# The final normalisation of a routed mixture-of-experts layer: one row tile in each expert step, the rest in one batch behind the steps

## What is computed

```python
y = fourier_mixer(x, w_in, w_out)
h = layer_norm(2 ** 0.25 * x + y, ln_g[0], ln_b[0])
scores = sigmoid(h @ w_router)
group = argmax(sum of the two best (scores + b_router) in each group of 8 experts)
two experts = top_k((scores + b_router)[group], 2);  gate = scores / their sum
y[token] = sum over its two experts e: gate * ((silu(h @ w_gate[e]) * (h @ w_up[e])) @ w_down[e])
out = layer_norm(2 ** 0.25 * h + y, ln_g[1], ln_b[1])
```

## Time and profile before

| | before |
|---|---|
| median of 3 runs | 2350.56 us |
| the profiled execution, and its span | 2350.37 us, 2348.4 us |
| TensorE busy | 2127.3 us (91%) |
| VectorE / ScalarE / GpSimd busy | 1373.1 / 998.2 / 582.7 us |
| HBM traffic | 436 MB, 186 GB/s over the span |

### The profile page before, as it was taken

The page is one execution under the profiler, slowest core; times in us unless marked ns, Lnnn a source line. Parts: engine busy times, 40 slices in busy tenths (PEclk is TensorE's granted clock), DMA queues, the critical chain, the costliest instruction groups (busy, mean ns, idle before and its releaser), DMA issues.

```text
span 2348.4 us, 37687 instructions
## 1 busy us (share of the span) xinstructions
PE 2127.3 (91%) x12222; PEld 1801.6 (77%) x12223; DVE 1373.1 (58%) x2254; ACT 998.2 (43%) x1442; POOL 582.7 (25%) x493
## 2 busy tenths in 40 slices
PE   8999899999999449999999999999999999999600
PEld 3443678888888349999999999999999999998500
DVE  3321148888887746555655656555555565555298
ACT  1221123333233226555555645655455565554143
POOL 1000034444544411211121121212111121211166
PEclk9999999999999769999999999999999999999855
DMA  6880233443333347767776866877677777766376
GB/s 226 283 287 21 67 126 113 147 147 125 116 127 108 126 153 210 222 203 195 219 216 184 248 194 211 227 223 197 180 220 218 219 218 228 209 202 183 98 286 238
DMA packets 136067, 435.59 MB, mean 185 GB/s; under 512 B 30912, under 2 KB 35008, under 8 KB 131904
## 3 DMA queue, kind: packets, MB, share of 16 engines
q1 hardware_dynamic: 98592, 307.12, 38.6%
q0 software_dynamic: 37440, 128.01, 21.6%
HBM read 328.01 MB, written 108.10 MB: 186 GB/s over the span
## 4 chain that ended last, share of the span: by engine, by line
PE 90%; POOL 3%; issue 3%; DMA 2%; DVE 2%; ACT 0%; SPq 0%; POOLq 0%; ACTq 0%; DVEq 0%
PE ps L877 36%; PE ps L901 15%; PE ps L759 15%; PE ps L696 5%; POOL fin_r L1689 3%; PE ps L865 3%; PE ps L741 3%; PE ps L909 2%; PE ps L715 2%; PE ps L793 2%; PE ps L650 1%; PE ps L780 1%; PE ps L700 1%; PE ps L870 1%; PE ps L659 1%
## 5 line engine op out<-in xcount | busy, mean ns | idle before, releaser
L901 PE MATMUL ps<-wd_hi,hidT 128*128 128x512 f32 x1056 | 293.0, 402 | 0.4 <-ACT hidT L1099 0.4
L1359 DVE TENSOR_TENSOR wd_lo<-wraw,wd_hi 128x1024 fp32r<-128x1024 f32 x132 | 161.9, 1226 | 199.0 <-ACT wd_hi L1057 198.7
L901 PEld LDWEIGHTS ps<-wd_hi,hidT 128*128 128x128 f32 x1056 | 190.1, 189 | 36.3 <-ACT hidT L1099 0.8
L1359 DVE TENSOR_TENSOR wg_lo<-wraw,wg_hi 128x1024 fp32r<-128x1024 f32 x132 | 161.4, 1224 | 92.6 <-ACT wg_hi L1057 92.5
L1632 POOL DMA_INDIRECT sums<-yrow_a,ent_now x33 | 57.2, 1733 | 558.4 <-DVE yrow_a L1422 515.4
L1359 DVE TENSOR_TENSOR wu_lo<-wraw,wu_hi 128x1024 fp32r<-128x1024 f32 x132 | 160.7, 1218 | 52.0 <-ACT wu_hi L1057 51.9
L877 PE MATMUL ps<-mxT_hi,wg_hi 128*128 128x256 f32 (+1 forms) x1056 | 163.3, 297 | 13.4 <-issue 13.4
L1099 ACT CAST hidT<-hid 128x320 fp32r<-128x320 f32 x132 | 60.7, 460 | 257.3 <-DVE hid L1440 257.3
L877 PEld LDWEIGHTS ps<-mxT_hi,wg_hi 128*128 128x128 f32 x1056 | 149.7, 191 | 17.9 <-issue 16.0
L877 PE MATMUL ps<-mxT_lo,wg_hi 128*128 128x256 f32 (+1 forms) x1056 | 163.2, 297 | 0.0
L877 PE MATMUL ps<-mxT_hi,wg_lo 128*128 128x256 f32 (+1 forms) x1056 | 162.6, 297 | 0.0
(11 more groups left out here) (212 smaller groups left out, 4120.0 us busy)
## 6 DMA issues: line engine op xcount, KB each, us to landing
wraw<-expert_w_gate SPq DMA_DIRECT2D x132, 512.0 KB, 5.4
wraw<-expert_w_up SPq DMA_DIRECT2D x132, 512.0 KB, 5.4
wraw<-expert_w_down SPq DMA_DIRECT2D x132, 512.0 KB, 4.4
xch<-x SPq DMA_DIRECT2D x16, 1024.0 KB, 6.7
first_stage<-ych SPq DMA_DIRECT2D x16, 1024.0 KB, 8.3
yt<-first_stage SPq DMA_DIRECT2D x16, 1024.0 KB, 4.9
fin_r<-sums SPq DMA_DIRECT2D x32, 512.0 KB, 3.9
out<-fin_r SPq DMA_DIRECT2D x32, 512.0 KB, 2.9
```

Of the source, the lines that this page charges most:

```text
L901: mm = nc.tensor.matmul(psY[h], hidT[:, l, c, t * P:(t + 1) * P], wd[r][:, c, cols], start=(i == c == 0), stop=(i == 2 and c == FC - 1))
L1359: nc.vector.tensor_tensor(piece(1, j), wraw[:, j % SLOTS, :], piece(0, j).bitcast(F32), ALU.subtract).then_inc(wlo_ok, 1)
```

## The change

1. The tokens of each group are written into a list too (four more lists, six list writes in place of four in list_tokens), and VectorE makes a second table (ltab) from the counts of the groups: for each step the number of row tiles that may be taken by then, and where each tile's list begins. The last tile of a group overlaps the one before it. The lists are laid out plainly (a list of 4480 entries for each expert and group) in place of by lanes, so the entries of a step come with three DMAs in place of four; there are 640 and 512 filler rows in place of 128 each.
2. In each step u one tile (lnrow) is normalised: SyncE loads its token numbers, GpSimd gathers its rows from sums in the step before and stores them to out at the end of its own work on the step before's entries; VectorE makes the statistics ahead of its down splits and gain and shift between them; ScalarE makes the root ahead of its first cast. Steps for which no tile is ready work on a dummy of filler rows.
3. The tiles that are left are done in batches of 10: GpSimd gathers all ten, VectorE does statistics and gain and, for even tiles, the shift; for odd tiles ScalarE scales and GpSimd adds the shift. GpSimd stores each by indirect DMA, after the store before it has landed.
4. In a step the second scatter no longer waits for the landing of the first.

```diff
-FB = 8
+LISTS = E + EG
+CAP = 35 * P
+FILL = 512
+FB = 10
...
@@ SyncE: start
-            sp.dma_start(acc[S:S + P, :], x[0:P, :]).then_inc(pad_out, 16)
-            sp.dma_start(hd[S:S + P, :], x[0:P, :]).then_inc(pad_out, 16)
+            sp.dma_start(acc[S:S + FILL + P, :], x[0:FILL + P, :]).then_inc(pad_out, 16)
+            sp.dma_start(hd[S:S + FILL, :], x[0:FILL, :]).then_inc(pad_out, 16)
...
@@ SyncE: expert steps
             load_entries(unit_row(sp, 1))
+            sp.dma_start(lng2, bcast(ln_g[1], P)).then_inc(ln2_in, 16)
+            sp.dma_start(lnb2, bcast(ln_b[1], P)).then_inc(ln2_in, 16)
+            sp.dma_start(lent_in_t, lists[E * CAP:E * CAP + P, :]).then_inc(lent_in, 16)
+            sp.wait_ge(ltab_ok, 1)
+            own_wait(sp, glist_out, 32 * GROUPS, sp_gate)
...
                     load_piece(u, e, j)
+                    if j == 0:
+                        tile = ln_slot(u)
+                        own_wait(sp, lent_ok, u, sp_gate)
+                        load_ln_tile(tile)
...
@@ TensorE: behind the step table
             mm.then_inc(utab_ps, 1)
+            pe.wait_ge(lcol_made, 1)
+            for k in range(2):
+                mm = nc.tensor.matmul(psLtab[:, k * P:(k + 1) * P], lcol[:, k:k + 1], ident,
+                                      start=True, stop=True)
+            mm.then_inc(ltab_ps, 1)
...
@@ ScalarE: a step
+            def ln_deviation(u):
+                act.wait_ge(lvar_ok, u + 1)
+                nc.scalar.activation(lnstd[:, 0:1], lnmv[:, 0, 1:2], ACT.Sqrt, bias=eps2_c).then_inc(lstd_ok, 1)
...
                 act.wait_ge(y1_ps, 2 * u + 2)
                 act.wait_ge(yc_ps, 2 * u + 2)
+                ln_deviation(u)
                 for k in range(FC):
                     split(u, GU_PIECES + k)
                     act.wait_ge(g_ps, 4 * u + k + 1)
...
@@ VectorE: a step
+            def ln_statistics(u):
+                dve.wait_ge(lrow_in, 16 * u + 16)
+                step.begin(unit_steps + LN_STEPS * u)
+                statistics(lnrow, 0).then_inc(lvar_ok, 1)
+
+            def ln_gain(u):
+                dve.wait_ge(lvar_ok, u + 1)
+                nc.vector.scalar_tensor_tensor(lnrow, lnrow, lnmv[:, 0, 0:1], lng2, ALU.subtract, ALU.mult
+                                               ).then_inc(lgain_ok, 1)
+                dve.wait_ge(lstd_ok, u + 1)
+                link(nc.vector.reciprocal(lnrs[:, 0:1], lnstd[:, 0:1]))
+
+            def ln_shift(u):
+                dve.wait_ge(lgain_ok, u + 1)
+                nc.vector.scalar_tensor_tensor(lnrow, lnrow, lnrs[:, 0:1], lnb2, ALU.mult, ALU.add
+                                               ).then_inc(lfin_ok, 1)
+
             def unit(u, more):
                 wide = unit_wide(dve, u)
-                for k in range(FC):
+                ln_statistics(u)
+                split(u, GU_PIECES)
+                ln_gain(u)
+                split(u, GU_PIECES + 1)
+                ln_shift(u)
+                for k in range(2, FC):
                     split(u, GU_PIECES + k)
...
@@ GpSimd: a step
+            def ln_gather(u):
+                if not is_first(u):
+                    own_wait(pool, lrow_out, 16 * u, pool_gate)
+                own_wait(pool, lent_in, 16 * u + 16, pool_gate)
+                nc.gpsimd.tensor_copy(lent, lent_in_t).then_inc(lent_ok, 1)
+                own_wait(pool, lent_ok, u + 1, pool_gate)
+                pool.indirect_dma_start(lnrow, None, acc, bass.IndirectOffsetOnAxis(ap=lent[:, 0:1], axis=0)
+                                        ).then_inc(lrow_in, 16)
+
+            def ln_store(u):
+                own_wait(pool, lfin_ok, u + 1, pool_gate)
+                pool.indirect_dma_start(out, bass.IndirectOffsetOnAxis(ap=lent[:, 1:2], axis=0), lnrow, None
+                                        ).then_inc(lrow_out, 16)
...
-                    if t:
-                        own_wait(pool, y_out, 32 * u + 16, pool_gate)
                     scatter(t, P, y_out)
...
                     own_wait(pool, entc_ok, u + 2, pool_gate)
+                    ln_store(u + 1)
                 if ahead == 2:
                     gathered(u + 2)
                     nc.gpsimd.tensor_copy(ent_next, ent_in).then_inc(ent_ok, 1)
                     own_wait(pool, ent_ok, u + 3, pool_gate)
+                    ln_gather(u + 2)
...
@@ VectorE and GpSimd: the batch at the end
+            with dve.Fori(0, batches(dve)) as i:
+                for b in range(FB + 1):
+                    if b < FB:
+                        normal(FB * i + b, i, b)
+                    if b:
+                        gain(FB * i + b - 1, b - 1)
+                    if b % 2:
+                        shift(FB * i + b - 1, b - 1)
...
+            with pool.Fori(0, batches(pool)) as i:
+                own_wait(pool, lents_in, 16 * FB * i + 16 * FB, pool_gate)
                 for b in range(FB):
-                    fin(FB * i + b, b)
+                    pool.indirect_dma_start(fin_r[:, b, :], None, acc,
+                                            bass.IndirectOffsetOnAxis(ap=lents[:, b, 0:1], axis=0)
+                                            ).then_inc(fin_in[b], 16)
+                for b in range(FB):
+                    if b:
+                        own_wait(pool, fin_out, 16 * FB * i + 16 * b, pool_gate)
+                    if b % 2:
+                        pool.wait_ge(fs_ok, FB // 2 * i + b // 2 + 1)
+                        nc.gpsimd.tensor_tensor(fin_r[:, b, :], fin_r[:, b, :], lnb2, ALU.add).then_inc(fp_ok, 1)
+                        own_wait(pool, fp_ok, FB // 2 * i + b // 2 + 1, pool_gate)
+                    else:
+                        own_wait(pool, fh_ok, FB // 2 * i + b // 2 + 1, pool_gate)
+                    pool.indirect_dma_start(out, bass.IndirectOffsetOnAxis(ap=lents[:, b, 0:1], axis=0),
+                                            fin_r[:, b, :], None).then_inc(fin_out, 16)
```

More of the change, by code:

```diff
@@ L39 @@
 PIECES, GU_PIECES = 12, 8
-FB = 8
+FB = 10
+MAX_LN = TILES + EG - 1
+LN_COLS = 80
 LB = 4
@@ L277, in trunk_kernel @@
         mid = keep.take("mid", CH * NG)
-        padl = keep.take("padl", 2 * USED_ROWS, I32)[0:LANES, :]
+        lent3 = keep.take("lent3", 6, I32)
+        lent_in_t, lent, pad_d = (lent3[:, 2 * i:2 * i + 2] for i in range(3))
+        lents_t = keep.take("lents", 2 * FB, I32)
+        pad_at = keep.byte / 1024
+        padl = [keep.take(n, 2 * CAP // P, I32) for n in ("pad_e", "pad_g")]
+        keep.take("ltab_end", 8)
+        ltab = at("ltab", pad_at, LANES + LN_COLS + 2, I32)[0:1, :]
         def small(name, *dims):
@@ L1498, in fin @@
-            def fin(t, i, b):
-                step.begin(start + 2 * t if is_first(t) else start + 2 * t - 1)
-                normal(t, i, b)
-                if not is_first(t):
-                    invert(t - 1, (b - 1) % FB)
-                if not is_first(t, 2):
-                    gain(t - 2, (b - 2) % FB)
-            start = step.start + step.k
-            for b in range(FB):
-                fin(b, 0, b)
-            with dve.Fori(1, TILES // FB) as i:
-                for b in range(FB):
-                    fin(FB * i + b, i, b)
@@ L1513, in _ @@
[L1513 to L1516 removed]
+                dve.wait_ge(fn_ok, t + 1)
+                nc.vector.scalar_tensor_tensor(fin_r[:, b, :], fin_r[:, b, :], lnmv[:, b % LB, 0:1], lng2,
+                                               ALU.subtract, ALU.mult).then_inc(fg_ok, 1)
+                dve.wait_ge(fstd_ok, t + 1)
+                nc.vector.reciprocal(lnrs[:, b % LB:b % LB + 1], lnstd[:, b % LB:b % LB + 1]).then_inc(fr_ok, 1)
```

301 lines of the change are left out of this document (174 added, 127 removed).

## The result

The changed kernel took 2361.55 us in the median of 17 runs (2358.56 to 2368.09), the kernel before, on the same chip, 2351.91 us (17 runs, 2346.83 to 2358.14). The ratio is 1.0043, with a 95% interval of 1.0035 to 1.0051. The change made the kernel 0.4% slower, within the half per cent that I had called no change. I had forecast 2332 us, a clear gain, so the sum was 30 us too low. The profiled execution took 2359.84 us; its span is 2358.1 us.

What follows compares the result with a forecast made beforehand. TensorE bounds the expert steps; a 137.6 us tail on the other engines follows. 2350.37 - 49 (tail) + 21.6 (stalls) + 9 (step 0) + 0.5 (two matmuls) = 2332.5, say 2332 us; range 2306 to 2368.

Steps and rivals of the forecast that it cites:

- The list writes: Row groups ahead of the steps: two more list writes per group on GpSimd, off TensorE's chain; forecast 0.
- Stalls in the steps: Expert steps: ScalarE waits for new statistics, so TensorE's third gate block waits for the first Silu; +21.6 us.
- Step 0: First expert step: dummy tile's late gather delays TensorE by 7.6 us, its lower clock adds 1.5; +9 us.
- The tail: After the last expert output: only ten tiles left, their end set by GpSimd's chain of stores; saves 49 us.
- Start and tables: Ahead of the steps: larger filler costs 0, at worst +10 us; the tile table's two matmuls +0.5 us.
- A: Whole kernel: the forecast itself, 2332 us, own range 2320 to 2345; chance 0.50, plus 0.04 with the start late.
- B: Expert steps: the first Silu isn't late, so only tail and step 0 count; 2310 us, chance 0.14.
- C: Expert steps: TensorE's granted clock falls at each of 16 stalls, 1.5 us each, +24; 2356 us, chance 0.10.
- D: Expert steps: the tile's scatter, store and gather round trip is late; with 1.5 us, 2380 us; chance 0.13.
- E: Tail: stores in the final chain land like accumulating ones, 10 x 2.24 us more; 2354 us, chance 0.08.
- F: Tail: an eleventh tile left makes a second batch of ten, +60 us; chance 0.01.

Runs made afterwards that it cites:

- before_lists: Kernel before plus only the two extra list writes per group of rows, to a tensor of their own, with their waits; 2374.26 us, ratio 1.0095.
- mix_early: Changed kernel with each group's two list writes issued one group later, where GpSimd waits for destinations anyway; 2346.58 us, ratio 0.9984.
- combo3: Changed kernel: early list writes, root behind fourth Silu, last shifts on VectorE, earlier dummy gather, last four groups' list writes in two later places; 2295.63 us.
- mix_none: Changed kernel without the two list writes per group, so all tiles of the last normalisation are filler; 2338.06 us, ratio 0.9945.
- step_late: Changed kernel with ScalarE's root behind its fourth Silu and VectorE's reciprocal and shift behind its four down splits; 2330.59 us, ratio 0.9916.
- mix_after: Changed kernel with the two list writes issued on GpSimd behind the stores of the rows (groups 2 to 14); 2385.45 us, ratio 1.0142.

## Why the prediction was wrong, step by step

**The list writes: zero forecast, 23 us measured; this is the step that failed.** I had written that GpSimd "waits there for VectorE's destinations and is no link of TensorE's chain, 0". GpSimd is no link by a wait, but signals of TensorE come late beside its issues, and the two writes moved its stores onto the end of a product whose signal is due at once. before_lists shows the price (22 us); mix_early (15 us back) and combo3 (the rest) show that the place makes it. Why the signals are late stays open. The second half of the sentence, "for the last group they are issued behind the four that SyncE waits for", is true of SyncE, which starts its loads 2.13 us behind the start of the fourth write in both kernels. It missed two things: the writes stand in front of GpSimd's own next gather (2.8 us), and ten issues come in a row around the last router product, and 7.2 us are lost from there to the last group's first list write (24.7 us; in mix_none, without the writes, that stretch takes 17.8 us, and 17.4 before).

**Stalls in the steps: 21.6 us forecast, 33.0 measured** (the sum of the 32 periods from one yrow_b to the next, against those of before). The mechanism was right: ScalarE's root stands ahead of the first Silu, and the third gate block waits for it; step_late takes it away. The chain was right too: 4.71 us from the start of VectorE's statistics to TensorE's third gate block (892.75 to 897.46, and 1351.34 to 1356.05), where I had 4.78 and 0.07, and eight narrow steps behind a narrow one grew by 1.5 to 1.6 us (forecast 1.77), 12.3 us together. The size failed for steps behind a wide one. I let the statistics begin as the last y_c ends; VectorE begins them 1.0 to 1.7 us later, for nothing that the profile names. So seven narrow steps behind a wide one grew by 1.6 to 2.1 us instead of 0.72, 12.8 us together, and nine wide ones by 0.7 to 1.2 us instead of nothing, 8.1 us together. Of the 32 periods 24 grew, and the Silu accounts for it: without step 0, TensorE's weight loads waited 32.0 us for it (37.7 less 5.7). The 0.5 us a narrow step that step_late keeps are not a part of this growth but a new wait of that edit, for hidT.

**Step 0: +9 forecast, +7.5 measured** (5.46 of waiting instead of 7.6, since the dummy's rows were in 8.3 us behind the first gate product instead of 10.0; the half clock behind the wait came as forecast).

**The tail: -49 forecast, -54.8 measured.** The first gather came as forecast (8.4 us behind the last copy, forecast 8.1), the ten gathers took 13.2 us (13). GpSimd went on 5.8 us behind the first store's issue (2296.83 to 2302.67), against 3.5 for a later one and the 10 that I had let it wait for the gathers ahead of it in the queue: 4 us. The Trainium skill (DMA: Bandwidth & Descriptors, "Two DMAs through the same engine are not ordered") says that within one queue of an engine descriptors start in order; the 2.3 us more than a later store agree with some waiting, the trace doesn't show how much of it is order. A store costs 4.45 us (forecast 4.6) and an odd tile 6.7 to 7.1 (7.7), so a pair 11.1 to 11.5 instead of 12.3: 3 us in all. Three passes of VectorE in the batch took 2.8 to 3.4 instead of 1.23 us beside GpSimd's addition, which I had kept as the upper bound; they were hidden.

**Start and tables: right.** The larger filler cost nothing up to 326 us, and the two matmuls of the tile table lie in front of a wait for the first rows.

**The rivals.** A, the forecast, failed through the terms above. B (Silu not late) is refuted by the 25 waits. C: the granted clock was 1.00 from 910 to 2200 us, through the stalls there; from 884 to 900 us, behind the pause ahead of step 0 and the one in it, it was 0.71. D: the tile's rows were late in step 0 only. E: a store's landing was seen 3.3 us behind the end of its issue, not 6. F: one batch of ten, as counted. The time fell between C's 2356 and D's 2380 us for a reason that none of them held; that it lay inside the range of 2306 to 2368 is luck. With the terms as measured, -54.8 for the tail, 40.6 for steps and step 0, 22.8 for the lists (from before_lists) and 1 for the rest ahead of the steps, the same sum gives 2350.4 - 54.8 + 40.6 + 22.8 + 1 = 2360 us.

## What to carry to other kernels

Cost an added DMA issue not only by who waits for it: look at what else is due in the microseconds in which it, and all that it pushes back on its engine, is issued, and give small writes a place where the engine waits anyway. Where a small operation joins an engine's queue, ask what stands behind it at a step's boundary; the same root behind the fourth Silu instead of ahead of the first was worth 31 us. A change whose gain is in one stage wants a list of everything that it adds in the other stages, with a price for each, even for two writes that wait for nobody.

## What the runs showed of the hardware

- Beside indirect DMA issues of GpSimd, TensorE's semaphore signals can reach ScalarE, SyncE and VectorE late, by up to 2.8 us (mix_after, 639.18 instead of 636.4), and then several at once. In the changed kernel the late copy begins 1.0 to 1.1 us behind the end of the last issue in 11 of 12 products; in the product shown of mix_after it is 1.35 us. It isn't the bytes: with 16 columns instead of 1024 the groups were as long. Not every issue does it. In the kernel before, four stores are issued beside the first half of the same product and no signal is late; in mix_none, with the stores in the same place to 0.2 us, the second signal is 0.3 to 0.5 us late and nothing is lost; in the changed kernel the first three signals of the product are late by 0.14 us at most and the fourth by 1.2 to 1.6. What decides it stays open.
- An indirect DMA issue on GpSimd, mostly 0.95 to 1.3 us, took 5.73 us for the last list write of the last group (5.73 in before_lists too, 5.1 in mix_early). VectorE's four splits of gate and up weights run beside it, and it ends 0.85 us behind the last of them: 859.28 against 858.43 in the changed kernel, 858.18 against 857.33 in before_lists, 841.81 against 840.96 in mix_early. In combo3 the first gather took 2.34 us beside two splits and ended 0.88 us behind them. That points to VectorE's splits and not to SyncE's loads, but no run moved them away.
- An operation of VectorE on 128 x 8 values took 5.23 us beside GpSimd's addition, in before_lists too (0.17 us otherwise; in the kernel before another operation met it, 5.42 us). The Trainium skill (SBUF — State Buffer, "SBUF: two separate sides") says that VectorE operations with two SBUF inputs and a GpSimd operation that reads SBUF exclude each other for the whole instruction; the trace agrees. Here it was a false trail: the operation had 4 us to spare, and the groups stayed long when the addition was moved back.
